# The gate's rows by VectorE's transpose and DRAM, and a third Strassen pair in a's projection

## The reference

```python
mod = (silu(c) @ w_ada + b_ada)[:, None, :]
shift, scale, gate = jnp.split(mod, 3, axis=-1)
h = rms_norm(x, g_norm) * (1 + scale) + shift
proj = h @ w_in                                   # seven parts of 1024 columns
a = silu(layer_norm(depthwise_conv31(v * sigmoid(gv)))) * silu(z)
b = (grouped(pooled_means(u) - u) * pool_scale) * silu(z2)
m = sigmoid(gate_a) * (a @ w_a_out) + sigmoid(gate_b) * (b @ w_b_out)
y = rms_norm(x + gate * (m @ w_out), g_final)
```

## Time and profile before

| | us |
|---|---|
| median of 3 runs | 919.33 (918.99 to 920.09) |
| the profiled execution | 918.88 |
| its span, first to last instruction | 917.1 |
| TensorE busy | 902.9 |
| VectorE busy | 797.5 |
| ScalarE busy | 414.1 |
| mean granted TensorE clock | 0.995 of full |

### The profile page before, as it was taken

One profiled execution on the slowest core, in us unless ns is written; L12 is line 12 of the kernel. 1 busy time (PEld: TensorE's weight loads), 2 busy tenths in 40 slices (PEclk: granted clock), 3 DMA queues, 4 the chain that ended last, 5 costly groups with the idle time before them and its releaser, 6 DMA issues.

```text
span 917.1 us, 17124 instructions
## 1 busy us (share of the span) xinstructions
PE 902.9 (98%) x7004; PEld 884.6 (96%) x7004; DVE 797.5 (87%) x915; ACT 414.1 (45%) x582; POOL 100.7 (11%) x109
## 2 busy tenths in 40 slices
PE   8999999999999999999999999999999999999996
PEld 5699999999999999999999999999999989999996
DVE  1797999997999996999997799999798798689767
ACT  5484354434453443454433445446434432436452
POOL 0122211111110201211111203000011000000000
PEclk9999999999999999999999999999999999999998
DMA  9879989889798979798888989648897662522515
GB/s 367 348 175 224 258 207 255 226 224 245 200 227 248 256 236 236 195 249 243 250 253 251 229 234 226 201 139 291 350 343 184 194 252 90 155 74 92 164 68 185
DMA packets 86366, 202.75 MB, mean 221 GB/s; under 512 B 12433, under 2 KB 19089, under 8 KB 82833
## 3 DMA queue, kind: packets, MB, share of 16 engines
q1 hardware_dynamic: 52960, 122.76, 38.7%
q0 software_dynamic: 22080, 52.46, 28.5%
q10 hardware_dynamic: 11248, 26.45, 8.1%
HBM read 175.67 MB, written 88.88 MB: 288 GB/s over the span
## 4 chain that ended last, share of the span: by engine, by line
PE 95%; DMA 2%; DVE 1%; SPq 1%; issue 0%; ACT 0%; DVEq 0%
PE ps L1080 23%; PE ps L1076 23%; PE ps L1074 23%; PE ps L1011 8%; PE ps L1014 8%; PE ps L1012 8%; DMA ada_raw<-w_ada 2%; PE ps L941 1%; PE ps L993 1%; PE ps L947 0%; PE ps L1272 0%; PE ps L1270 0%; PE ps L1269 0%; DVE bf L1821 0%; DVE hf L2374 0%
## 5 line engine op out<-in xcount | busy, mean ns | idle before, releaser
L2012 DVE SCALAR_TENSOR_TENSOR conv_y<-conv_u,par_all,conv_y 128x1024 f32<-128x1024 f32 x240 | 301.1, 1284 | 2.1 <-DVE conv_y L1998 0.6
L1076 PE MATMUL ps<-tr,hr 128*128 128x258 f32 x824 | 216.4, 283 | 0.0
L1074 PE MATMUL ps<-tr,hr 128*128 128x258 f32 x824 | 215.4, 283 | 0.0
L1466 ACT ACTIVATE hr<-raw 128x512 fp32r<-128x512 f32 (+1 forms) x188 | 115.9, 618 | 116.1 <-PE ps L1080 87.5
L1080 PE MATMUL ps<-tr,hr 128*128 128x258 f32 x824 | 166.4, 283 | 0.0
L1076 PE MATMUL ps<-hr 128*128 128x258 f32 x616 | 161.5, 283 | 0.0
L1074 PE MATMUL ps<-hr 128*128 128x258 f32 x616 | 160.8, 282 | 0.0
L1074 PEld LDWEIGHTS ps<-tr,hr 128*128 128x128 f32 x824 | 156.9, 190 | 0.0
L1076 PEld LDWEIGHTS ps<-tr,hr 128*128 128x128 f32 x824 | 155.7, 189 | 0.0
L1891 DVE TENSOR_TENSOR hr<-raw,hr 128x512 fp32r<-128x512 f32 (+1 forms) x188 | 126.5, 677 | 5.5 <-ACT hr L1466 1.6
L1080 PEld LDWEIGHTS ps<-tr,hr 128*128 128x128 f32 x824 | 127.3, 188 | 0.0
(11 more groups left out here) (289 smaller groups left out, 1581.5 us busy)
## 6 DMA issues: line engine op xcount, KB each, us to landing
w_sums<-w_main POOLq DMA_DIRECT2D x64, 512.0 KB, 9.5
raw<-w_sums SPq DMA_DIRECT2D x120, 256.0 KB, 4.5
raw<-w_main SPq DMA_DIRECT2D x94, 256.0 KB, 4.8
w_sums<-w_sums POOLq DMA_DIRECT2D x30, 512.0 KB, 5.8
w_sums<-w_main ACTq DMA_DIRECT2D x26, 512.0 KB, 5.5
ada_raw<-w_ada SPq DMA_DIRECT2D x8, 1024.0 KB, 21.1
w_raw<-w_main SPq DMA_DIRECT2D x16, 512.0 KB, 5.7
bf<-x_t SPq DMA_DIRECT2D x4, 1032.0 KB, 8.1
```

Of the source, the lines that this page charges most:

```text
L1074: nc.tensor.matmul(bank[:, c, :], wh[:, w_cols], x_hi[:, k, t_cols], start=start and k == 0, stop=False, skip_group_check=True)
L1076: nc.tensor.matmul(bank[:, c, :], wh[:, w_cols], x_lo[:, k, t_cols], start=False, stop=False, skip_group_check=True)
L1466: nc.scalar.activation(ring(q)[0][:, 0:n], raw5[:, raw_slot(q), 0:n], ACT.Copy).then_inc(item_hi, 1)
L2012: ins = v.scalar_tensor_tensor(out=y, in0=conv_u[:, x, k:k + SEQ], scalar=par_all[:, g, x, k:k + 1], in1=y, op0=ALU.mult, op1=ALU.add)
```

## The change

There are five edits.
- `gate_turn` and `gate_out` are gone. VectorE transposes the gate's bank in 32x32 blocks into SBUF (`gate_transpose`). SyncE stores the nine columns of each of the four row groups to DRAM (`store_gate`, 4 DMAs) and loads them back with the parts of one channel beside one another (`load_gate_parts`, 4 DMAs). VectorE adds the four parts with a reduction and then the bias (`gate_modulation`). This happens for both halves of the gate.
- a's projection has two plain tiles (0 and 1) and three pairs: A_A (2 and 3), A_B (4 and 5), A_C (6 and 7), with an order of 21 forms of its own. P5 of the first pair waits for the second transpose, because both use the same bank. The weight sums have one chunk more, with OUT_B alone in it.
- JOB_A_LAST and its splits are gone, and M_ORDER ends with tiles 7 and 6, which come from P4 and P3 of A_C.
- The weights of the four plain output tiles (0, 1, 7, 6) go through the ring of blocks as two halves each (W0, W1), with `ring_step` in place of `k_step`. P1 of OUT_B waits for the first third of tile 1's result and no longer for all of it.
- The two fillers at the end (WARM_FINAL) are gone.

The core of the diff:

```diff
-A_ITEMS = [("P1", A_A), ("P1", A_B), ("P6", A_A), ("P2", A_A), ("P7", A_A), ("P5", A_A), ("P6", A_B), ("P4", A_A), ("P3", A_A),
-           ("P2", A_B), ("P7", A_B), ("P5", A_B), ("P4", A_B), ("P3", A_B)]
+A_ITEMS = [("P1", A_A), ("P1", A_B), ("P5", A_A), ("P2", A_A), ("P6", A_A), ("P2", A_B), ("P7", A_A), ("P6", A_B), ("P4", A_A), ("P3", A_A),
+           ("P7", A_B), ("P1", A_C), ("P5", A_B), ("P4", A_B), ("P3", A_B), ("P6", A_C), ("P5", A_C), ("P7", A_C), ("P2", A_C),
+           ("P4", A_C), ("P3", A_C)]
-M_ORDER = [0, 1, 2, 4, 3, 6, 5, 7]
+M_ORDER = [0, 1, 3, 2, 5, 4, 7, 6]
...
+            def store_gate(n):
+                sp.wait_ge(gate_rows_ready, n + 1)
+                rows = gate_rows[:].rearrange("p (b r n) -> p b r n", b=ADA_BLOCKS, r=QUADS)
+                for r in range(QUADS):
+                    sp.dma_start(t["gate_rows"][n, r], rows[:, :, r, 0:NMOD]).then_inc(gate_stored, 16)
+
+            def load_gate_parts(n):
+                sp.wait_ge(gate_stored, 16 * QUADS * (n + 1))
+                for r in range(QUADS):
+                    parts = t["gate_rows"][n, r].rearrange("(q j) b n -> j q (b n)", q=QUADS)
+                    sp.dma_start(gate_parts[n][r * QUAD:(r + 1) * QUAD].rearrange("p q b n -> p q (b n)"), parts).then_inc(gate_parts_loaded[n], 16)
...
             single(JOB_A, a_hi, a_lo, before_k=lambda k: pe.wait_ge(a_lo_done, k + 1))
             gate_chunk(0)
             single(JOB_A + 1, a_hi, a_lo)
-            gate_turn(0)
             gate_chunk(1)
-            single(JOB_A + 2, a_hi, a_lo)
-            gate_turn(1)
...
                 if form == "P5":
                     pe.wait_ge(c12_out, n)
-                    pe.wait_ge(gate_ready, 2)
+                    pe.wait_ge(gate_rows_ready, 2)
                     a_t_product(i, form, n, bank_c, start=True)
...
-            pe.wait_ge(c21_out, A_B + 1)
-            job(JOB_A_LAST % 2, a_hi, a_lo, before_k=last_a)
...
+            pe.wait_ge(c21_out, A_C + 1)
+            plain_out(0, M_ORDER)
+            pe.wait_ge(c11_out, A_C + 1)
+            plain_out(1, range(KT))
...
-                    pe.wait_ge(dve_evac, FIRST_STRASSEN - 1 + (n - OUT_A) - JOB_B)
+                    if n == OUT_A:
+                        pe.wait_ge(dve_evac, JOB_OUT + 1 - JOB_B)
+                    else:
+                        pe.wait_ge(first_bank_out, 1)
...
             token_columns(2, sq_sum, start=False, stop=False)
-            keep_warm(WARM_FINAL, 0)
...
+            def gate_transpose(n):
+                dve.wait_ge(gate_done, n + 1)
+                if n:
+                    dve.wait_ge(gate_stored, 16 * QUADS * n)
+                v.transpose(gate_rows[:], aux[:, n, :]).then_inc(gate_rows_ready, 1)
+
             def gate_modulation(n):
-                dve.wait_ge(gate_turned, n + 1)
-                v.tensor_tensor(mod[:, 4 + n, :, :], aux[:, n, 0:ADA_BLOCKS * NMOD].rearrange("p (j n) -> p j n", j=ADA_BLOCKS),
-                                wide(ada_b[:, 4 + n, :], NMOD), ALU.add).then_inc(gate_ready, 1)
+                dve.wait_ge(gate_parts_loaded[n], 16 * QUADS)
+                gate = mod[:, 4 + n, :, :]
+                link(v.tensor_reduce(gate, gate_parts[n].rearrange("p q b n -> p b n q"), AX_X, ALU.add))
+                link(v.tensor_tensor(gate, gate, wide(ada_b[:, 4 + n, :], NMOD), ALU.add))
```

More of the change, by code:

```diff
@@ L798, in _ @@
             sp.wait_ge(m_full, 2)
             load_sig_a(5)
[L800 to L807, removed]
+            load_gate_parts(0)
+            for i in range(6, 10):
+                load_block(i)
@@ L808, in _ @@
+            store_gate(1)
+            for i in range(10, 13):
+                load_block(i)
+            load_gate_parts(1)
+            for i in range(13, 17):
+                load_block(i)
             sp.wait_ge(m_full, M_ORDER.index(3) + 1)
             load_sig_a(7)
[L810 to L815, removed]
@@ L846, in _ @@
             load_x(3)
-            for i in range(4, len(OUT_ITEMS)):
-                load_out_item(i)
+            for i in range(OUT_RING + 4, OUT_RING + len(OUT_ITEMS)):
+                load_block(i)
             sp.wait_ge(x_new_ready, 3)
@@ L1274, in _, with plain_out @@
-            last.then_inc(pe_done, 1)
-            single(JOB_OUT + 1, m_hi, m_lo)
+            m_hi, m_lo = [gr[:, k, :] for k in range(KT)], [gr[:, KT + k, :] for k in range(KT)]
+            def plain_out(m, order):
+                for j, k in enumerate(order):
+                    if j % KH == 0:
+                        pe.wait_ge(item_lo, A_SPLIT + RING_AT["W0" if k < KH else "W1", m] + 1)
+                    pe.wait_ge(m_lo_done, M_ORDER.index(k) + 1)
+                    last = ring_step(m, k, m_hi[k], m_lo[k], j == 0, j == KT - 1)
+                    if j % KH == KH - 1:
+                        last.then_inc(item_done, 1)
@@ L1569, in _ @@
                     tap0(*TAP0_AT[slot])
[L1570 removed]
+                if form == "P1" and n % 2 == 0 and n // 2 + 2 < SUM_CHUNKS - 2:
                     first_sums(n // 2 + 2)
@@ L2151, in a_result @@
                 first, second = HALVES
-                if form not in ("P2", "P5", "P4", "P3"):
+                c22 = i == max(A_AT["P5", n], A_AT["P7", n])
+                if form not in ("P2", "P4", "P3") and not c22:
                     return
@@ L2205, in _ @@
             dve.sem_inc(t_summed, 1)
+            gate_transpose(1)
+            link(v.scalar_tensor_tensor(out=at4, in0=at2, scalar=-1.0, in1=br[:, upper_k, first].bitcast(F32), op0=ALU.mult, op1=ALU.subtract))
             a_t_lo("P6", 2)
[L2207 to L2214 removed]
@@ new lines, in _ @@
+                if (form, n) == ("P2", A_B):
+                    a_t_lo("P4", 4)
+                if (form, n) == ("P5", A_C):
+                    m_split_lo(0)
+                if (form, n) == ("P7", A_C):
+                    m_split_lo(1)
+                if (form, n) == ("P2", A_C):
+                    m_split_lo(3)
+                if (form, n) == ("P4", A_C):
+                    for m in (2, 5, 4):
+                        m_split_lo(m)
+            m_split_lo(7)
+            m_split_lo(6)
@@ L2311, in _ @@
             dve.sem_inc(t_summed, 1)
-            dve.wait_ge(gate_ready, 2)
+            for n in range(2):
+                gate_modulation(n)
             v.tensor_scalar(minus_gate[:], mod[:, 4:6, :, 0], -1.0, None, ALU.mult)
```

386 lines of the change are left out of this document (166 added, 220 removed).

## The result

| | before | after |
|---|---|---|
| median of 5 runs, us | 918.99 (917.89 to 920.09) | 926.60 (925.47 to 928.57) |
| the profiled execution | 918.88 | 925.48 |
| its span | 917.1 | 923.4 |
| mean granted TensorE clock | 0.995 | 0.993 |

The ratio is 1.0086 with a 95% interval of 1.0074 to 1.0098. The change makes the kernel slower by 0.9%; the 926.60 us are 7 over the forecast and outside the range.

A forecast was written before the change was run, and what follows sets the result against it. TensorE, busy 98% of the span, was taken as the bound. −4.24 + 3.15 (VectorE late in a's pairs) + 1.75 − 0.45 = +0.2 us on 918.88 gave 919.1, plus 0.45 for the median: 919.5 us, range 916.6 to 922.2.

The forecast's parts named there:

- TensorE's own work: Gate turns and a's projection: two turns removed, −1.58 us, and two plain tiles made a pair, −2.66; sum −4.24.
- The transpose: VectorE's gate transposes ahead of P5 in a's first pair: taken as 0.60 us each, without a row.
- P5's wait of 1.4 us: a's first pair: P5 waits for the second transpose to free its bank, starting at 761.4, +1.4 us.
- The price of 1.2 at P2 and 0.5 at P4: a's pairs: VectorE's gapless chain makes TensorE wait 1.2 us at the second pair's P2 and 0.5 at P4.
- DMA and queues: Gate stores and loads, ring blocks, extra weight sums and TensorE's gate chunk: all hidden, no term in the sum.
- five us and more of room: First four gate stores: issued about 749, asked for by the second transpose at 760.6; nearest store row lands in 5.1 us.
- Block 6 lands in some 4.5 us: hidden: Ring load behind the gate stores on SyncE: issued near 759.4, needed by VectorE at 769.2, so no cost.
- the stores are late: Second transpose: past 11.6 us from 749, each further us costs TensorE one; 922.9 at 15; chance 0.17, shared with slow transpose.
- The hand-over to the output tiles: From a's last forms to tiles 7 and 6: TensorE does not wait, slack 0.35 and 0.6 us.
- The second place: Output pairs, where VectorE must keep up: waits of 0.75 us at P1, 0.8 at P7, 0.2 at P4; together +1.75.
- The end: Column sums at the end: removing the fillers starts the root sooner, −0.45 us, bounds 0 and −0.55.
- The turn against a rule: Gate turns: by the skill's rule moving them to VectorE gains nothing; by TensorE's row alone 1.58 us.

The follow-up runs named there:

- Experiment 7: Changed kernel with the gate turned on TensorE, fillers back and VectorE's order mended, three pairs kept; 917.57 us, ratio 0.9978 to the kernel before.
- experiment 1: Changed kernel with a buffer of its own for the second transpose; 925.07 us, ratio 1.0058 to the kernel before.
- experiment 3: Changed kernel with each gate chunk stored by one DMA of whole 2 KB rows and 32 small loads behind block 12; 931.69 us, ratio 1.0126 to before.
- experiment 5: Kernel before with the gate's part of the change alone, three plain tiles, two pairs and fillers kept; 922.22 us, ratio 1.0028 to before.
- experiment 2: Changed kernel with a buffer of its own for the second transpose and the first half's part loads moved behind block 12; 921.77 us, ratio 1.0024 to before.
- experiment 4: Changed kernel with the gate's part undone, turns on TensorE, three pairs kept and no fillers; 918.15 us, ratio 0.9987 to the kernel before.
- experiment 6: Kernel before without the two fillers at the end, nothing else; 918.66 us against 919.13, ratio 0.9989.
- 8: As Experiment 7, but the gate by DRAM with two buffers, its stores one by one behind blocks 6 to 13; 918.86 us, ratio 0.9989 to before.

## Why the prediction was wrong

By its own steps.

- **TensorE's own work**, −4.24 us: right. In a's stretch the difference is +4.51; less the wait (7.23 from 760.31, when TensorE could have gone on, to 767.54) and the 1.3 of P5's slow clock it is −4.0. Experiment 7 gives 2.47 for the third pair alone, against 2.66.
- **The transpose**, 0.60: 0.63. VectorE was laid out to come to the second at 760.6 and came at 760.69. P5's wait of 1.4 us appeared as 1.3 and 1.4 in experiments 1 and 3, where the stores don't hold the transpose. The price of 1.2 at P2 and 0.5 at P4 never showed in the changed kernel: TensorE was 6 us late by then. In experiment 3, where no store is waited for, P2 waits 0.8 and P4 not at all.
- **DMA and queues**: this is the step that failed, in the sentence "five us and more of room", by which the sum has no term for the stores. It sized four stores of 512 runs of 36 bytes by the row of a store of 15 KB that lands in 5.1 us. They took 17.75 us from the first issue to the last landing. That row was of about the same size in KB, and was chosen for its short runs, but it told nothing of four such stores one behind another: these take 11.60 us even in experiment 5, which uses up all the room. Nor did it tell of full DMA engines. The third pair's weight sums, which the same step calls hidden since they are read late, are under way in the same engines, and the other 6.2 us go with them. "Block 6 lands in some 4.5 us: hidden" fails too: behind the short runs, blocks of 256 KB took 11.28 us in experiment 2 and 7.18 in experiment 5, and without short runs ahead the same blocks took 5.76 and 2.67.
- **The rival** "the stores are late" named the mechanism, the place and the threshold of 11.6 us from 749. By its rule, 17.6 us would give 919.5 + 6.0 = 925.5; the median is 926.60. Its chance was put at 0.17, from a single row, and its far end at 15 us. It left out the clock after the wait, +1.3, and counted the waits at P2 and P4 besides, which go, −1.7.
- **The hand-over to the output tiles**, no wait: right, 22.73 us against 22.72.
- **The second place**, +1.75: +1.86, with waits of 0.8 at P1 (forecast 0.75) and 0.5 for a low part of the weights at P7 (forecast 0.8 there and 0.2 at P4). Counted from start to start the two cost 0.98 and 0.64, so that the sum is closer than its terms. The gate's four small ops take 1.4 us, the forecast had 1.0. In experiment 4, without them, the same stretch loses 0.8 us; in 7, with the order mended, nothing.
- **The end**, −0.45: −0.36 here and −0.31 in experiment 6.
- **The turn against a rule**: the rule of the Trainium skill (VectorE: DVE Perf Modes, Rules for kernel authors), TensorE for a full 128x128 transpose and VectorE for 32x32 blocks, came out right in its verdict. The 0.63 us on VectorE was no dearer than said; what four row groups of 32 need behind a block transpose, the sum across groups, went by way of DRAM here, and that is where the 8.4 us are.

## What to carry to other kernels

Before data goes by way of DRAM, count its runs, not its bytes, and look at what else the DMA engines carry then: the landing time of one small store in a quiet place is no price for four of them in a busy one (5.1, 11.6 and 17.75 us here). Traffic that is itself "hidden", since it is read late, still makes other transfers late. A buffer that a DMA still reads is a wait like any other, and a buffer of one's own only moves it, if a queue that feeds others waits for the same store. A fraction of a us on the bounding engine is worth keeping where its replacement puts traffic ahead of loads that this engine needs.

## What the hardware showed that was not expected

- With four stores of 512 runs of 36 bytes under way, the share of the 16 DMA engines from 757 to 766.5 us was 1.10 at 67 GB/s; without them (experiment 4) it was 0.72 at 197. SyncE was held 3.14 us at the issue of the third (L804 at 750.13), and no more than 0.66 at any of them in experiment 5, where less else was under way. One store of 128 runs of 2 KB, 256 KB, landed in 10.0 us (experiment 3). The Trainium skill (DMA: Bandwidth & Descriptors, Specifications) says that runs under 512 bytes don't reach the line rate, since the memory is read, changed and written for them. The rows agree with the first half; nothing here shows the mechanism. The prediction did not weigh this rule, and should have.
- After TensorE had stood for 7 us it ran at 1.2 GHz (0.50 of full) for the next 2.7 us, 1.3 us lost. Shorter stalls cost too: the clock was 0.66 in 775 to 780 us after the 4.3 us of experiment 1, and 0.83 in 785 to 795 us after the 2.0 of experiment 5, where it fell to 0.50 only when TensorE had been running again for 0.6 us. Behind the waits of 1.3 and 1.5 us for the transpose in experiments 1 and 2 it stayed at 1.00. The Trainium skill (TensorE: Matmul & The Clock Gate, What's actually happening) tells of two levels, the lower one after TensorE has been idle. The traces agree, with these numbers. In these kernels a wait of 2.0 us or more on the bounding engine was thus dearer than its length by 1.3 to 1.6 us, as far as P2, P4 and P5 were looked at.
- At the end of the program, where TensorE has small matmuls and gaps, the clock falls in some kernels before the spread is done and in others after it. The eight matmuls of the spread took 1.11 us in before, after and experiment 7, 1.19 in 6, 1.40 in 1, 1.49 in 2, 1.89 in 3, and 2.0 in 4, 5 and 8. With the fillers there are both 1.11 and 2.0, without them as well, so they don't decide it. What does was not found, and it is 0.9 us, as much as some of the effects above.
